# Attention value group of a head issued directly behind the turn of its slot, ahead of the slot's second share of gate parts

## The reference, cut to what matters

```
gates  = sigmoid(x @ w_gate + b_gate)                 # 3 groups of 1024 channels
# B, one head: causal softmax over 512 keys
s  = (q_h @ k_h.T) * scale ; s = where(causal, s, -inf)
pr = softmax(s) ; y_b[h] = pr @ v_h
# A, one head: the same with one k and v for all heads, and only the
# top 128 keys of each query (chosen by an indexer) left in the softmax
merged = gates[0]*(y_a @ wb0) + gates[1]*(y_b @ wb1) + gates[2]*(y_c @ wb2)
```

## Time and profile before

| | us |
|---|---|
| median of 3 runs | 1783.97 |
| the profiled execution, its own time | 1783.46 |
| its span, first to last instruction | 1781.7 |
| PE busy in the span | 1756.3 (99%) |
| DVE busy | 1287.4 (72%) |
| ACT busy | 966.0 (54%) |
| POOL busy | 818.6 (46%) |

### The profile page before, as it was taken

One profiled execution on the slowest core, in us unless ns is written; L12 is line 12 of the kernel. 1 busy time (PEld: TensorE's weight loads), 2 busy tenths in 40 slices (PEclk: granted clock), 3 DMA queues, 4 the chain that ended last, 5 costly groups with the idle time before them and its releaser, 6 DMA issues.

```text
span 1781.7 us, 29532 instructions
## 1 busy us (share of the span) xinstructions
PE 1756.3 (99%) x10254; PEld 1547.4 (87%) x10254; DVE 1287.4 (72%) x2503; ACT 966.0 (54%) x1905; POOL 818.6 (46%) x464
## 2 busy tenths in 40 slices
PE   9999999999999999999999999999999999999997
PEld 9888888878889999988898888888787899999886
DVE  6379988867799888713363899887778988887033
ACT  4544777844475565622244557787444665555222
POOL 5446943354434333354434578434443334334542
PEclk9999999999999999999999999999999999999999
DMA  5332111223332323233333321112233332322331
GB/s 192 103 92 91 60 60 60 62 74 103 95 118 96 119 96 107 84 119 106 95 97 104 97 84 60 60 60 63 80 107 95 102 112 98 117 96 95 118 99 67
DMA packets 47082, 166.69 MB, mean 94 GB/s; under 512 B 5472, under 2 KB 5728, under 8 KB 46944
## 3 DMA queue, kind: packets, MB, share of 16 engines
q1 hardware_dynamic: 46080, 163.60, 28.8%
q10 hardware_dynamic: 864, 1.28, 0.2%
HBM read 162.76 MB, written 2.10 MB: 93 GB/s over the span
## 4 chain that ended last, share of the span: by engine, by line
PE 89%; DVE 6%; ACT 2%; issue 2%; POOL 1%; DVEq 0%; ACTq 0%; POOLq 0%
PE banks L1161 23%; PE banks L1163 23%; PE banks L1162 23%; PE banks L1213 4%; PE banks L1215 4%; PE banks L1214 4%; PE banks L1269 2%; PE banks L1316 2%; DVE sb_xl L1874 1%; DVE banks L1709 1%; DVE sb_u L1867 1%; PE banks L1300 1%; PE banks L1245 1%; PE banks L1299 0%; DVE sb_u L1837 0%
## 5 line engine op out<-in xcount | busy, mean ns | idle before, releaser
L622 POOL TENSOR_TENSOR sb_wl<-sb_wraw,sb_wh 128x1024 fp32r<-128x1024 f32 x205 | 500.6, 2445 | 613.9 <-ACT sb_wh L750 588.1
L1161 PE MATMUL banks<-sb_xh,sb_wh 128*128 128x512 f32 (+1 forms) x1152 | 405.8, 352 | 4.3 <-DVE banks L2133 1.5
L1163 PE MATMUL banks<-sb_xh,sb_wl 128*128 128x512 f32 (+1 forms) x1152 | 389.2, 338 | 0.0
L1162 PE MATMUL banks<-sb_xl,sb_wh 128*128 128x512 f32 (+1 forms) x1152 | 388.4, 337 | 0.0
L750 ACT ACTIVATE sb_wh<-sb_wraw 128x1024 fp32r<-128x1024 f32 x199 | 210.2, 1057 | 267.2 <-PE banks L1163 160.1
L1161 PEld LDWEIGHTS banks<-sb_xh,sb_wh 128*128 128x128 f32 x1152 | 219.3, 190 | 25.5 <-issue 6.4
L1163 PEld LDWEIGHTS banks<-sb_xh,sb_wl 128*128 128x128 f32 x1152 | 218.7, 190 | 24.3
L1162 PEld LDWEIGHTS banks<-sb_xl,sb_wh 128*128 128x128 f32 x1152 | 219.6, 191 | 13.5
L1161 PE MATMUL banks<-sb_t_hi,sb_wh 128*128 128x256 f32 x768 | 217.6, 283 | 2.8 <-ACT sb_u L1088 2.0
L1162 PE MATMUL banks<-sb_t_lo,sb_wh 128*128 128x256 f32 x768 | 217.3, 283 | 0.0
L1163 PE MATMUL banks<-sb_t_hi,sb_wl 128*128 128x256 f32 x768 | 217.3, 283 | 0.0
(11 more groups left out here) (348 smaller groups left out, 4048.4 us busy)
## 6 DMA issues: line engine op xcount, KB each, us to landing
sb_wraw<-in_weights SPq DMA_DIRECT2D x256, 512.0 KB, 3.6
sb_wraw2a<-in_weights SPq DMA_DIRECT2D x24, 512.0 KB, 3.7
sb_wraw2b<-in_weights SPq DMA_DIRECT2D x24, 512.0 KB, 4.5
sb_u<-in_x SPq DMA_DIRECT2D x8, 256.0 KB, 6.5
out<-sb_u SPq DMA_DIRECT2D x8, 256.0 KB, 2.1
sb_praw<-in_ple ACTq DMA_DIRECT2D x2, 512.0 KB, 4.2
sb_par<-in_params ACTq DMA_DIRECT2D x2, 98.5 KB, 2.5
sb_rope_tmp<-in_freq ACTq DMA_DIRECT2D x1, 24.0 KB, 4.3
```

The source lines that it names most:

```text
L622: nc.gpsimd.tensor_tensor(wl[:, t % WS, :], wraw[:, t % 2, :], wh[:, t % WS, :].bitcast(F32), ALU.subtract).then_inc(lo_ready, 1)
L1161: nc.tensor.matmul(out, wh_, xh_, start=start, stop=False, skip_group_check=onto)
L1162: nc.tensor.matmul(out, wh_, xl_, start=False, stop=False, skip_group_check=onto)
L1163: return nc.tensor.matmul(out, wl_, xh_, start=False, stop=stop, skip_group_check=onto)
```

## The change

In `attention_steps()`, in a slot with a value group, the step ("value", head) is appended right behind the step ("turn", ...), ahead of the second share of parts; ("value part", head), which only ACT executes, stays where it was.

```
         if TURN_LAG <= slot < UNITS + TURN_LAG:
             steps.append(("turn", slot - TURN_LAG))
+        if whole:
+            steps.append(("value", head))
         steps += [("part", p) for p in left[given + shares[0]:given + shares[0] + shares[1]]]
         if slot in PREP and PREP[slot][0] == "B":
             steps.append(("prep keys", PREP[slot]))
-        if whole:
-            steps.append(("value", head))
         if whole:
             steps.append(("value part", head))
```

## The result

| | before | after |
|---|---|---|
| median of 11 runs, us | 1783.97 (1783.33 to 1785.33) | 1788.68 (1787.52 to 1790.23) |
| the profiled execution, us | 1783.46 | 1788.89 |
| its span, us | 1781.7 | 1787.1 |

The changed kernel is slower: ratio 1.0028, 95% interval 1.002 to 1.0035, which is 3.6 to 6.2 us. Forecast was 1788.7.

The account below looks back on a forecast made before the run. PE was taken to bound the kernel, attention stages included. Head losses of 2.37 us per layer, 4.74 for both, on the profiled 1783.46 gave 1788.2; plus 0.51 to the median, 1788.7 us, range 1786.2 to 1791.3.

Parts of the forecast that it names:

- heads 0 to 2, together: First three heads of a layer: VectorE is late by its own work, and PE loses 0.47 us in all.
- head 8: Value group of head 8: its low half ends behind the turn, so PE loses 0.55 us per layer.
- head 10: Value group already waits and keeps its time; the part now comes behind it, a loss of 0.70 us per layer.
- head 12: Value group of head 12: its low half ends behind the turn, so PE loses 0.55 us per layer.
- head 13: Value group of head 13: its low half ends just behind the turn, a loss of 0.10 us per layer.
- price by starts: PE's stalls counted between instruction starts, 4.74 us in all, instead of by the idle column, 2.96 us.
- E - T + 0.08: A stalled head's loss in us: E, end of its last line 1683; T, start of the first pass behind the turn.
- The early loss counts once: Heads 0 to 2: 0.47 us paid once, not three times, since PE's delay eats its waits for `q_l`.
- Nothing comes back through `pt_l`: VectorE may start the next head up to 0.70 us sooner, but gains nothing past the next mask's wait for PE's score.
- the first: Rival: VectorE's head start reaches the late low halves of heads 8, 10 and 12; about 1784.9 us, chance 0.15.
- the second: Rival: faster, because freeing the single `pt_l` earlier removes PE's four waits per layer; down to 1779.8 us, chance 0.05.
- The third: Rival: worse, PE's stalls push VectorE back, each early head pays and near misses lose; 1791.2 us, chance 0.12.

Follow-up runs that it names:

- kernel 1: The change only at heads 3, 4, 5, 6, 7, 9, 11, 13, 14, 15, the other six as before: 1783.92 us, before 1783.55.
- kernel 3: The change at heads 8, 10 and 12 only, the others as in the kernel before: 1787.21 us, before 1783.55.
- kernel 2: The change at heads 0, 1 and 2 only, the others as in the kernel before: 1784.82 us, before 1783.55.
- kernel 7: The changed kernel with six early VectorE convolution taps moved to slots 14, 18, 22, 26, 30 and 42: 1783.87 us, before 1783.56.
- kernel 6: The kernel before with six early VectorE convolution taps moved to slots 14, 18, 22, 26, 30 and 42: 1781.51 us, before 1783.56.
- kernel 4: The changed kernel with VectorE's single-tap slots moved from 28, 43, 58 to 36, 44, 52, before A preps: 1787.77 us, before 1783.55.
- kernel 8: The kernel before with six early VectorE taps moved and head 10's value group one part later: 1780.04 us, before 1783.56.

## Why the prediction was right

By its own terms, layer 1. "Measured" is the growth of the delay from head to head: how much later the pass behind the group and its part starts than the corresponding pass of the kernel before, less what was there at the last head.

| term | predicted, us | measured, us |
|---|---|---|
| heads 0 to 2, together | 0.47 | 0.68 |
| head 8 | 0.55 | 0.52 |
| head 10 | 0.70 | 0.68 |
| head 12 | 0.55 | 0.55 |
| head 13 | 0.10 | none |
| all others | 0 | -0.09 |
| stage | 2.37 | 2.34 |

The stage agrees to 0.03 us, and the forecast with the median to 0.02, partly by luck: heads 0 to 2 were 0.21 too small, and head 13, the others and the two small differences at heads 8 and 10 together 0.24 too large. The mechanism held in every term but head 13's:

- **PE bounds the stage and the move has no price of its own**: shown by kernel 1. One sign of it was worded too strongly: PE's busy time in the stage of layer 1 was to be unchanged and rose from 219.02 to 219.92 us, for the reason given under "price by starts".
- **Each stall is E - T + 0.08**: right within 0.03 us at heads 8, 10 and 12. Kernel 3 alone gives their sum.
- **The early loss counts once**: right in kind (kernel 2), 0.2 us too small. Two small things were missed. The groups of heads 0 to 2 start 0.14 us after the low half's end, not 0.06, so that head 0 alone loses 0.50; and "VectorE does not wait for PE there" fails once, which adds 0.17 at head 2. Before and after:

```profile
198.98 0.68 DVE L1668 CUSTOM_DVE_ANT_0 sb_pbuf<-banks,sb_causal 128x512 f32<-128x512 f32 x1
```

```profile
199.98 0.69 DVE L1668 CUSTOM_DVE_ANT_0 sb_pbuf<-banks,sb_causal 128x512 f32<-128x512 f32 x1
```

  This mask, in slot 11, is 1.00 us later in the trace, where VectorE's work at head 1 was 0.85 later (194.51 to 195.36), nearly all of it the 0.87 from ahead of the stage. It now begins 0.61 us behind the start of the score's last pass (199.37), as masks do that wait for their score, where before it began 0.96 behind. The low half of head 2 carries the delay on: 1.02 us later (207.77 to 208.79).
- **Head 13** lost nothing: its low half came later by 2.92 us where PE's turn came later by 3.21, so that the group no longer had to wait. Kernels 1 and 3 tell whence: in kernel 1, without the stall of head 12 ahead of it, head 13 does lose its 0.11; in kernel 3, where heads 8, 10 and 12 alone are moved, its low half ends 0.27 us before the pass behind the turn, as against 0.03 after it in the kernel before. Behind head 12's group, in slot 55, VectorE was 0.35 us behind PE's score before and in kernel 1, and is not in kernel 3 and the change. That is absorption, which I had counted as none.
- **Nothing comes back through `pt_l`**: right for this kernel. Before head 8 VectorE's wait moved from the group to the score: where the earlier trace rows show 1.27 us and then 0.25, it is now 0.59 and then 0.93, the same sum:

```profile
272.85 0.29 DVE L1683 TENSOR_TENSOR sb_pt_l<-banks,sb_pt_h 128x128 fp32r<-128x128 f32 x1 [0.59 <-PE banks L1316]
...
274.79 0.69 DVE L1668 CUSTOM_DVE_ANT_0 sb_pbuf<-banks,sb_work 128x512 f32<-128x512 f32 x1 [0.93 <-PE banks L1300]
```

  It holds as long as the next mask waits for its score. Kernel 7 shows where it ends: with an extra tap VectorE is late there, and the earlier group gives 0.44 us a stage back.
- **Price by starts, not by the idle column**: the new waits ahead of line 1316 show 0.25 us at head 8, and 0.49 were lost (0.52 behind the turn's start against 0.03). With the idle column the sum would have been 2.96; the stages grew by 4.60. As the Trainium skill says in Perfetto Trace Analysis (Tensor Engine Instruction), the end of a matmul in the profile is an estimate. The trace agrees: passes that follow each other every 0.23 us are shown as 0.39 to 0.40 us long. A wait therefore shows short by what it lays bare of the last pass, and that part is booked as busy.
- **Rivals**: the first and the second fall with kernels 1 and 3, since groups moved early gave nothing back alone or together with this placing of the taps; what PE's other waits needed was VectorE's own work moved (kernel 6) and not `pt_l` freed sooner. The first rival's mechanism exists, though: kernel 7 shows it at work. The third falls with kernel 2.

One reason given was only half right: why heads 8 and 12 are late. The prediction put it on the 7.9 us of VectorE's work alone; kernel 4 shows that without that work ScalarE's copies would hold the low half up to within 0.14 us of the same moment. The forecast did not rest on it, an attempt to mend it did.

## What to carry to other kernels

On an engine that bounds the stage, work that waits for nobody is cover, and its place is directly ahead of the instruction whose input comes last. Before moving a group, list for each repetition when its input ends and when the engine would reach it: here ten of sixteen were free to move and six made the whole cost. Bringing forward what other engines wait for helps only if the engine that bounds waits for them in turn; here VectorE carried its earliness no farther than its next wait for PE's score. It was worth something only where VectorE had so much work that it no longer waited there (kernel 7). And of two chains that end almost together the profile names one; shortening it gains only their distance (kernel 4).

## What the hardware showed that I had not expected

A wait of PE for VectorE cost 0.17 to 0.24 us more from start to start than the idle time shown (0.43 against 0.26 in the earlier trace rows, 0.49 against 0.25 at head 8 of the change); in kernel 8 0.17 us were lost with none shown. From the end of VectorE's write to PE's first pass it took 0.06 us at heads 8, 10 and 12 and 0.14 us at heads 0 to 2, each time and in both layers; why it differs is open.
